# A two-block transformer kernel: the final norm and the next block's norm become one row, and column sums are asked for later

## The chip, the cores and the metric

The kernel runs on one core of one Trainium2 chip. The metric is the device time of one execution in microseconds. The core has five engines with their own instruction queues: PE (TensorE, matmuls out of SBUF into the eight banks of PSUM), DVE (VectorE), ACT (ScalarE), POOL (GpSimd) and SP, which here only issues DMAs. Engines are ordered against each other by semaphores: an instruction waits until a counter has reached a value, and everything behind it on its engine waits with it.

## The reference, cut to what matters

x has T = 512 tokens of D = 1024 features. The first block is an FFN, a mixer of attention and a linear recurrence, and a second FFN, each ahead of an RMS norm, and one final norm. The second block normalises that result once more and projects it ten ways.

```python
def rmsnorm(x, g):
    y = x * rsqrt(mean(x * x, axis=-1) + EPS)
    return y * g
...
x = x + 0.5 * swiglu_ffn(rmsnorm(x, ffn1_norm), ...)
x = x + hybrid_mixer(rmsnorm(x, mix_norm), ...)
x = x + 0.5 * swiglu_ffn(rmsnorm(x, ffn2_norm), ...)
x = rmsnorm(x, final_norm)          # the first block's result
...
h = rms_norm(x, norm_pre_g)         # the second block
u_a, z_a, q, k, v, o, z_b, gates, g_a, g_b = split(h @ w_in)
y_a = pool_mix(multiscale_pool(u_a)) * pool_scale * silu(z_a)
q, k = silu(conv5(q, k))
hb = mlstm(q, k, v, gates) + flip(mlstm(flip(...)))
y_b = rms(hb) * mlstm_norm_g * sigmoid(o) * silu(z_b)
merged = sigmoid(g_a + b_a) * (y_a @ w_proj_pool) + sigmoid(g_b + b_b) * (y_b @ w_proj_mlstm)
return x + rms_norm(merged @ w_out, norm_post_g)
```

## The kernel before

**Layout.** Everything is held transposed: features on the 128 partitions in 8 chunks, the 512 tokens along the row. So a norm's sum over features goes across partitions. It is done by ACT squaring the chunks into `scr`, DVE adding them (`add_square`, L1518, or `norm_sum`, L1506), PE turning the sums into four columns by narrow matmuls with a column of ones (`add_squares`, L494), ACT taking the root, DVE the reciprocal (`r_col`), and PE spreading it again as a row over all partitions (`spread_columns`, L501), which ACT copies to `r_row`.

**Weight units.** All weights come as 262 units of 128x1024 fp32 (512 KB). For each, SP issues the DMA (L414), ACT rounds it to `w_hi` (`head`, L1067), POOL subtracts for the rest `w_lo` (L432), and PE runs 24 matmuls of 128x512 columns: hi times hi, hi times lo, lo times hi over 8 chunks (`tile_unit`, L486 to L488; in the FFNs' second half `down`, L566 to L568). Each of the three buffers has two slots, so ACT's copy for unit u + 2 waits until PE has ended unit u. The stream x is split alike into `h_hi` (ACT, L1086) and `h_lo` (DVE, L1513).

**Norms 0 to 2** (before FFN1, the mixer, FFN2) multiply only the gain onto the stream; the root row is multiplied onto the results as they leave PSUM (L1552, L1556 in the FFNs). PE runs the first unit of the stage, then the column sums, the second unit, the row of roots, and goes on. **Norms 3 and 4** (the final norm, and the second block's) are done in full before PE goes on: x times gain times row (DVE, L2118), again squares, pair sums on POOL (L457), sums, root, row, and the normalised stream's split by DVE (L1539, L1535) and POOL (L450). Then the gates unit runs.

**Second block, in program order.** The gates unit (rows of gate values for the recurrence, prefix scans on DVE, L1805 ff.); `mlstm(0)`: ten head units whose results ACT copies out of PSUM (`take`, L1333), four convolutions on DVE (L1884, L1886) each followed by ACT's activation (L1341); a loop of three rounds `mlstm(h)`, in which the recurrence of head h - 1 (scores, eight steps with `c_state`, L1950, `roots`, `gated`, `y_tail`, L1988) runs between the ten units of head h; a last round with eight gate units (U_GB, L1402) between; `merge_b` (8 units); `pooled` (8 units for u, L1439, 8 for z, L1445, 2 for the mixing, L1019); `merge_a` (16); `output` (8, L2078). The order on each engine is written out by hand in these functions; nothing reorders it. Then the post norm (norm 5) of the output, and DVE (L2086, L2093) and POOL (L472, the first five chunks) multiply and add it to x, which SP writes out in eight DMAs.

## Time and profile before

| | |
|---|---|
| median of 3 runs | 1795.54 us (1794.02 to 1796.08) |
| the profiled execution, its own time | 1797.42 us |
| its span, first to last instruction | 1795.6 us |
| busy: PE, DVE, POOL, ACT | 1693.2, 700.0, 656.1, 623.7 us |
| mean granted TensorE clock | 0.969 |
| read from HBM | 144.86 MB, 82 GB/s over the span |

PE is busy 94% of the span. A busy time is a sum of the engine's instructions; where PE has a gap, the profile names what released it. The clock is the share of full speed (2.4 GHz) that was granted; it has two levels, 1.00 and 0.5, and a value between is a mean over a stretch. Matmul starts at full clock follow each other by 0.227 us, each shown with 0.39 us since they overlap.

### The profile page before, as it was taken

How to read it: one execution, taken by the hardware profiler on the slowest of the kernel's cores; microseconds unless marked ns; L12 is line 12 of the kernel's file. 1: busy time of each engine (PE TensorE's matmuls, PEld its weight loads, DVE VectorE, ACT ScalarE, POOL GpSimd, SP SyncE). 2: the span in 40 equal slices, each digit the busy share in tenths (PEclk: the TensorE clock that was granted, in tenths of full speed). 3: DMA queues.
4: the chain of work that ended last, by engine and by line, in shares of the span. 5: the costliest groups of instructions: out<-in, count | busy, mean ns of one | idle time of the engine just before them, and what ended most of it. 6: DMA issues, size and time to landing. Idle time of an engine off the chain costs nothing.

```text
span 1795.6 us, 22547 instructions
## 1 busy us (share of the span) xinstructions
PE 1693.2 (94%) x7996; PEld 1384.5 (77%) x7996; DVE 700.0 (39%) x1157; ACT 623.7 (35%) x917; POOL 656.1 (37%) x281
## 2 busy tenths in 40 slices
PE   6999999999999999999999988889898999999997
PEld 5888888778886678888888877677677778877876
DVE  4333330225326744333330127473736331463223
ACT  4332231234236653223321234334343423234431
POOL 2444444433330024444444434222222223444443
PEclk9999999999999999999999989899999999999998
DMA  3322232233220002222222222121111112322221
GB/s 145 103 95 93 94 103 95 94 140 94 82 82 25 2 33 85 94 97 101 93 93 96 103 71 71 59 71 59 58 58 58 58 59 82 117 93 88 100 94 70
DMA packets 41663, 148.68 MB, mean 83 GB/s; under 512 B 4624, under 2 KB 4752, under 8 KB 41360
## 3 DMA queue, kind: packets, MB, share of 16 engines
q1 hardware_dynamic: 40112, 142.36, 23.4%
q10 hardware_dynamic: 1504, 5.66, 1.0%
q8 instruction: 32, 0.52, 0.1%
q14 instruction: 15, 0.12, 0.0%
HBM read 144.86 MB, written 2.10 MB: 82 GB/s over the span
## 4 chain that ended last, share of the span: by engine, by line
PE 47%; issue 39%; POOL 9%; DVE 3%; ACT 1%; POOLq 0%; DVEq 0%; ACTq 0%
PE ps L486 10%; PE ps L488 10%; PE ps L487 10%; POOL w_lo L432 9%; PE ps L566 3%; PE ps L568 3%; PE ps L567 3%; PE ps L724 1%; PE ps L494 1%; PE ps L736 1%; PE ps L746 1%; PE ps L501 1%; DVE scr L1518 1%; PE ps L647 0%; DVE scr L2068 0%
## 5 line engine op out<-in xcount | busy, mean ns | idle before, releaser
L432 POOL TENSOR_TENSOR w_lo<-w_raw,w_hi 128x1024 fp32r<-128x1024 f32 x262 | 636.1, 2428 | 1001.9 <-ACT w_hi L1067 992.4
L486 PE MATMUL ps<-h_hi,w_hi 128*128 128x512 f32 x1504 | 600.6, 399 | 25.7 <-POOL w_lo L432 20.7
L1067 ACT ACTIVATE w_hi<-w_raw 128x1024 fp32r<-128x1024 f32 x260 | 275.5, 1060 | 945.5 <-PE ps L488 763.5
L487 PE MATMUL ps<-h_lo,w_hi 128*128 128x512 f32 x1504 | 592.0, 394 | 0.0
L488 PE MATMUL ps<-h_hi,w_lo 128*128 128x512 f32 x1504 | 591.6, 393 | 0.0
L486 PEld LDWEIGHTS ps<-h_hi,w_hi 128*128 128x128 f32 x1504 | 287.2, 191 | 90.8 <-issue 22.1
L488 PEld LDWEIGHTS ps<-h_hi,w_lo 128*128 128x128 f32 x1504 | 286.3, 190 | 61.1
L487 PEld LDWEIGHTS ps<-h_lo,w_hi 128*128 128x128 f32 x1504 | 286.8, 191 | 58.9
L566 PE MATMUL ps<-hid_hi,w_hi 128*128 (+1 forms) x352 | 137.2, 390 | 1.8 <-POOL w_lo L432 1.8
L567 PE MATMUL ps<-hid_lo,w_hi 128*128 (+1 forms) x352 | 136.9, 389 | 0.0
L568 PE MATMUL ps<-hid_hi,w_lo 128*128 (+1 forms) x352 | 136.9, 389 | 0.0
L1556 DVE TENSOR_TENSOR silu<-ps,r_row 128x512 f32<-128x512 f32 x44 | 30.4, 692 | 205.7 <-PE ps L488 201.8
L1571 DVE SCALAR_TENSOR_TENSOR x<-ps,x 128x512 f32<-128x512 f32 x16 | 11.0, 690 | 207.4 <-PE ps L568 207.4
L1561 DVE TENSOR_TENSOR hid_lo<-hid,hid_hi 128x512 f32 x44 | 71.1, 1615 | 40.1 <-ACT hid_hi L1116 40.1
L566 PEld LDWEIGHTS ps<-hid_hi,w_hi 128*128 128x128 f32 x352 | 66.1, 188 | 15.8 <-issue 2.2
L567 PEld LDWEIGHTS ps<-hid_lo,w_hi 128*128 128x128 f32 x352 | 66.1, 188 | 13.8
L568 PEld LDWEIGHTS ps<-hid_hi,w_lo 128*128 128x128 f32 x352 | 66.1, 188 | 13.8
L1886 DVE SCALAR_TENSOR_TENSOR scr<-qk_pad,param,scr 128x512 f32<-128x512 f32 x64 | 60.0, 938 | 7.7 <-DVE scr L1884 1.8
L1552 DVE TENSOR_TENSOR silu<-ps,r_row 128x512 f32<-128x512 f32 x44 | 30.4, 691 | 71.2 <-PE ps L488 54.1
L486 PE MATMUL ps<-y_hi,w_hi 128*128 128x512 f32 x128 | 50.0, 391 | 0.8 <-DVE y_lo L2043 0.7
L487 PE MATMUL ps<-y_lo,w_hi 128*128 128x512 f32 x128 | 49.8, 389 | 0.0
L488 PE MATMUL ps<-y_hi,w_lo 128*128 128x512 f32 x128 | 49.8, 389 | 0.0
(291 smaller groups left out, 1653.0 us busy)
## 6 DMA issues: line engine op xcount, KB each, us to landing
w_raw<-in_units SPq DMA_DIRECT2D x262, 512.0 KB, 3.2
x<-in_x SPq DMA_DIRECT2D x4, 512.0 KB, 7.1
w<-in_w ACTq DMA_DIRECT2D x1, 2048.0 KB, 8.1
out<-x SPq DMA_DIRECT2D x8, 256.0 KB, 2.0
scr<-proj ACTq DMA_DIRECT2D x8, 128.0 KB, 2.4
inv_count<-in_inv_count ACTq DMA_DIRECT2D x1, 1024.0 KB, 5.1
const<-in_const SPq DMA_DIRECT2D x1, 770.0 KB, 10.3
q_sc<-in_row_const ACTq DMA_DIRECT2D x1, 512.0 KB, 3.6
```

Source lines behind the costliest of these rows:

```text
L432: nc.gpsimd.tensor_tensor(w_lo[:, slot, :], w_raw[:, slot, :], w_hi[:, slot, :].bitcast(F32), ALU.subtract).then_inc(w_lo_done, 1)
L486: nc.tensor.matmul(ps[:, bank, :], whi, hi[:, k, :], start=(n == 0), stop=False)
L487: nc.tensor.matmul(ps[:, bank, :], whi, lo[:, k, :], start=False, stop=False)
L488: mm = nc.tensor.matmul(ps[:, bank, :], wlo, hi[:, k, :], start=False, stop=(n == DC - 1))
L566: nc.tensor.matmul(acc, w_hi[:, slot, at:at + P], mv_hi, start=start and kk == 0, stop=False)
L567: nc.tensor.matmul(acc, w_hi[:, slot, at:at + P], mv_lo, start=False, stop=False)
L568: mm = nc.tensor.matmul(acc, w_lo[:, slot, at:at + P], mv_hi, start=False, stop=stop and kk == 1)
L1067: nc.scalar.activation(w_hi[:, slot, :], w_raw[:, slot, :], ACT.Copy).then_inc(w_hi_done, 1)
L1552: nc.vector.tensor_tensor(silu[:, f, :], ps[:, 4 + 2 * f, :], r_row[:, :], ALU.mult).then_inc(scaled_done, 1)
L1556: chain.link(nc.vector.tensor_tensor(silu[:, f, :], ps[:, 5 + 2 * f, :], r_row[:, :], ALU.mult))
L1561: nc.vector.tensor_tensor(hid_lo[:, at, :].rearrange("p a t -> p (a t)"), hid[:, f, :], hid_hi[:, at, :].rearrange("p a t -> p (a t)").bit ...
L1886: ins = nc.vector.scalar_tensor_tensor(acc, tap, w, acc, ALU.mult, ALU.add)
```

## The change

In seven parts:

1. **Start.** The first gains come in a DMA of their own, and ACT loads its function table by a dummy copy before the data arrive. PE's first unit runs its w_hi matmuls first and w_lo's behind them.
2. **Norms 0 to 2.** PE runs two units before the column sums (in FFN and mixer), and a third before the row of roots. In the FFN's second half ACT copies w_hi for the next unit ahead of the squares, and the half-way sums on PE go.
3. **Norms 3 and 4** are one: the stream of the second FFN's result is x times the product of both gains (`both_col`), and the row for it is worked out from two sets of column sums, of the squares and of the squares weighed with the final gain's square (`root_of_both`, `inverse_of_both`). POOL's part in the norm goes.
4. **Second block's results.** Each leaves PSUM by a DVE multiply with the row (`take`, `take_gate`), ACT's functions then work in SBUF in place.
5. **x for the residual.** The normalised x, no longer formed above, is made in `pooled`: ACT multiplies a chunk with the gain, PE transposes it, ACT copies it back as token rows with the tokens' factor.
6. **Output** is computed with the tokens on the partitions: blocks of `m_hi`, `m_lo` are the stationary side and untiled w_out the moving one, over all eight banks, the chunk outermost.
7. **Post norm** is then a sum along the row: ACT squares with an accumulated sum, root, DVE reciprocal and multiply with a row of gains. POOL adds six pieces instead of five.

The diff, cut to its core:

```diff
@@ PE
+            def first_unit(bank, chunks):
+                pe.wait_ge(w_hi_done, 1)
...
             def column_sums(n):
                 pe.wait_ge(sqsum_done, n + 1)
...
+                bank = 5 if n == 3 else 0
+                mm = add_squares(bank, 0, scr[:, 0, :], True, True)
+                if n == 3:
+                    mm = add_squares(bank, TT, r_row, False, True)
+                mm.then_inc(ssq_done, 1)
...
-                            if first and f == 0:
-                                (row_of_roots if m else column_sums)(norm_of)
+                            if first and (f, m) == (0, 1):
+                                column_sums(norm_of)
+                            elif first and (f, m) == (1, 0):
+                                row_of_roots(norm_of)
...
-                if sums_inside:
-                    squares_of_half(norm_of + 1, True)
...
-                    if u == 0:
+                    if u == 1:
                         column_sums(1)
-                    elif u == 1:
+                    elif u == 2:
                         row_of_roots(1)
...
             def pooled():
-                with pe.Fori(0, DC) as i:
+                for j in range(DC):
+                    pe.wait_ge(ev_done, EV_POOL + j + 1)
+                    tile_unit(unit(U_POOL + j), 2 + j % 2, h_hi, h_lo)
...
+                    pe.wait_ge(xg_done, j + 1)
+                    for tt in range(TT):
+                        mm = nc.tensor.transpose(ps[:, 4 + j % 4, tt * P:(tt + 1) * P], x[:, j, tt * P:(tt + 1) * P], ident)
+                    mm.then_inc(xt_ready, 1)
...
             def output():
+                for k in range(DC):
+                    u, _, slot = unit(U_OUT + k)
+                    pe.wait_ge(w_lo_done, u + 1)
+                    pe.wait_ge(m_lo_done, k + 1)
+                    for tt in range(TT):
...
-            norm(3, "before")
-            norm(4, "last")
             gates()
@@ ACT
                 streams(0, 4)
+                head(unit(ud + kps + 2))
                 squares(norm_of + 1, 0, 4)
-                head(unit(ud + kps + 2))
...
                 for j in range(DC):
                     head(unit(U_POOL + j + 2))
...
-                    nc.scalar.activation(u_pad[:, j % 2, 8:8 + T], ps[:, 2 + j % 2, :], ACT.Copy).then_inc(ev_done, 1)
+                    nc.scalar.activation(x[:, j, :], x[:, j, :], ACT.Copy, scale=p_("g_final", j, j + 1)).then_inc(xg_done, 1)
                     if j >= 1:
                         pool_head(j - 1)
+                    act.wait_ge(xt_ready, j + 1)
+                    for tt in range(TT):
+                        at = slice(tt * P, (tt + 1) * P)
+                        ins = nc.scalar.activation(x[:, j, at], ps[:, 4 + j % 4, at], ACT.Copy, scale=x_col[:, tt:tt + 1])
...
+                for tt in range(TT):
+                    act.wait_ge(out_done, tt + 1)
+                    nc.scalar.activation(merged[:, 2 * (tt % 2):2 * (tt % 2) + 2, :], ps[:, 2 * tt:2 * tt + 2, :], ACT.Square,
+                                         accum_out=g_col[:, tt:tt + 1]).then_inc(osq_done, 1)
@@ DVE
+                def take(j):
+                    dve.wait_ge(unit_done, U_HEADS + HEAD_UNITS * h + j + 1)
...
+                    nc.vector.tensor_tensor(dst, ps[:, head_bank(j, not core), :], r_row[:, :], ALU.mult).then_inc(ev_done, 1)
...
+                between = take if units else lambda j: [take_gate(i) for i in GATE_B_AT[j]]
...
+                between(3)
+                step(0)
...
+                gated()
+                run(not units, (take_gate, 6), (take_gate, 7))
+                y_tail()
...
+                for n, (tt, half) in enumerate(PIECES):
...
+                    nc.vector.scalar_tensor_tensor(scr[:, n, :], ps[:, n, :], r_col[:, tt:tt + 1], g_row[:, half * T:(half + 1) * T],
                                                    ALU.mult, ALU.mult).then_inc(sum_done, 1)
```

**DVE, end of `mlstm(0)`**, the head units' stage between the gate scans and the loop. L1884 and L1886 (L1921 and L1923 after) are a convolution, L1895 (L1932) a product of gates, L1863 to L1868 (L1878 to L1883) the gate rows' products and columns. Before:

```order
L1858 TENSOR_SCALAR q_sc<-q_sc 64x512
L1884 TENSOR_SCALAR scr<-qk_pad,param 128x512 [waits qk_done,ev_done]
L1886 SCALAR_TENSOR_TENSOR scr<-qk_pad,param,scr 128x512 [waits dve_chain] x4
L1884 TENSOR_SCALAR scr<-qk_pad,param 128x512 [waits qk_done,ev_done]
L1886 SCALAR_TENSOR_TENSOR scr<-qk_pad,param,scr 128x512 [waits dve_chain] x4
L1895 TENSOR_TENSOR merged<-merged,scr 128x512 [waits ev_done]
```

After:

```order
L1873 TENSOR_SCALAR q_sc<-q_sc 64x512
L1904 TENSOR_TENSOR scr<-ps,r_row 128x512 [waits unit_done]
L1921 TENSOR_SCALAR scr<-qk_pad,param 128x512 [waits qk_done,ev_done]
L1923 SCALAR_TENSOR_TENSOR scr<-qk_pad,param,scr 128x512 [waits dve_chain] x4
L1904 TENSOR_TENSOR merged<-ps,r_row 128x512 [waits unit_done] x2
L1921 TENSOR_SCALAR scr<-qk_pad,param 128x512 [waits qk_done,ev_done]
L1923 SCALAR_TENSOR_TENSOR scr<-qk_pad,param,scr 128x512 [waits dve_chain] x4
L1904 TENSOR_TENSOR scr<-ps,r_row 128x512 [waits unit_done]
```

The evictions (L1904) of units 6 and 7 stand between the third and the fourth convolution, which came one behind the other before.

**ACT in `pooled`**, one of the eight u units. L1067 (L1088 after) is the w_hi copy for the unit after next, L1430 (L1444) the split of a pooled chunk. Before:

```order
L1067 ACTIVATE w_hi<-w_raw 128x1024 [waits unit_done,raw_full0]
L1439 ACTIVATE u_pad<-ps 128x512 [waits pool_done,unit_done]
L1430 ACTIVATE y_hi<-scr 128x512 [waits pool_done]
L1067 ACTIVATE w_hi<-w_raw 128x1024 [waits unit_done,raw_full1]
L1439 ACTIVATE u_pad<-ps 128x512 [waits pool_done,unit_done]
```

After:

```order
L1088 ACTIVATE w_hi<-w_raw 128x1024 [waits unit_done,raw_full0]
L1448 ACTIVATE x<-x,param 128x512
L1444 ACTIVATE y_hi<-scr 128x512 [waits pool_done]
L1454 ACTIVATE x<-ps,x_col 128x128 [waits xt_ready]
L1454 ACTIVATE x<-ps,x_col 128x128 x3
L1088 ACTIVATE w_hi<-w_raw 128x1024 [waits unit_done,raw_full1]
```

The eviction of u has left ACT; the scaled copy of x stands behind the w_hi copy, and PE's transposes wait for it; the copies back wait for PE.

**DVE in the head loop**, from the end of the third convolution to the first step's state copy (`c_state`). Before:

```order
L1886 SCALAR_TENSOR_TENSOR scr<-qk_pad,param,scr 128x512
L1901 ISA
L1902 REGISTER_ALU [waits cadd_ready]
L1902 TENSOR_SCALAR k_w<-k_tok,wk_tok 128x256
L1946 ISA [waits cadd_ready]
L1950 COPY c_state<-ps 128x257 [waits num_ready]
```

After:

```order
L1923 SCALAR_TENSOR_TENSOR scr<-qk_pad,param,scr 128x512
L1891 REGISTER_ALU
L1895 REGISTER_ALU [waits unit_done]
L1904 TENSOR_TENSOR qk_pad<-ps,r_row 128x512 [waits conv_done]
L1938 ISA
L1939 REGISTER_ALU [waits cadd_ready]
L1939 TENSOR_SCALAR k_w<-k_tok,wk_tok 128x256
L1983 ISA [waits cadd_ready]
L1987 COPY c_state<-ps 128x257 [waits num_ready]
```

The fourth eviction (unit 3 of the next head) stands between the third convolution and the step; three more stand ahead of earlier parts of the round.

## Rows read from the trace of the kernel before

**Rows 1.** The page, part 1: engine, busy us, share of the span, instructions
```profile
PE 1693.2 (94%) x7996; PEld 1384.5 (77%) x7996; DVE 700.0 (39%) x1157; ACT 623.7 (35%) x917; POOL 656.1 (37%) x281
```

**Rows 2.** Windows by stage: start:end and length, busy us (instructions), clock, DMA
```profile
1059.21:1088.18 28.97, 19.21 (x94) 16.43 (x92) 18.14 (x29) 12.39 (x21) 10.27 (x7) 0.65 0.07 21
1088.18:1162.42 74.24, 64.07 (x271) 51.62 (x272) 43.46 (x56) 30.72 (x39) 24.52 (x11) 0.91 0.24 78
...
1248.41:1338.94 90.53, 79.55 (x348) 65.69 (x349) 46.43 (x99) 31.75 (x46) 24.07 (x10) 0.94 0.17 58
...
1541.45:1631.93 90.48, 87.70 (x385) 71.78 (x384) 48.41 (x47) 31.45 (x42) 39.69 (x17) 1.00 0.32 109
...
1776.66:1795.60 18.94, 6.43 (x47) 6.05 (x47) 9.46 (x13) 0.89 (x2) 6.61 (x5) 0.62 0.30 111
```

**Rows 3.** Windows over single units and behind gaps, same columns
```profile
395.78:402.88 7.10, 7.10 (x27) 5.80 (x28) 0.18 (x1) 0.27 (x1) 0.00 (x0) 0.79 0.17 61
702.02:709.33 7.31, 7.31 (x28) 5.89 (x28) 0.18 (x1) 0.26 (x1) 1.50 (x1) 0.77 0.37 133
335.69:342.50 6.81, 6.81 (x30) 5.66 (x31) 0.00 (x0) 1.04 (x1) 2.26 (x1) 1.00 0.47 154
1145.36:1152.20 6.84, 6.84 (x23) 5.53 (x24) 0.00 (x0) 0.77 (x2) 2.37 (x1) 0.75 0.45 156
```

**Rows 4.** Timeline of the start: start us, us, engine line, what [idle before]
```profile
9.47 7.77 DVE L1513 SCALAR_TENSOR_TENSOR h_lo<-x,param,h_hi 128x512 fp32r<-128x512 f32 x6 [0.67 <-ACT h_hi L1086]
...
24.44 1.86 PE L494 MATMUL ps<-const,scr 128*128 128x1 f32 x8 [4.92 <-DVE scr L1518]
```

**Rows 5.** Timelines of PE at the first half-way step and two norms
```profile
335.69 0.49 PE L566 MATMUL ps<-hid_hi,w_hi 128*128 x1 [1.83 <-POOL w_lo L432]
...
394.66 1.26 PE L494 MATMUL ps<-const,scr 128*128 128x1 f32 x8 [4.28 <-DVE scr L1518]
...
701.11 1.05 PE L494 MATMUL ps<-const,scr 128*128 128x1 f32 x8 [1.18 <-DVE scr L1518]
```

**Rows 6.** Timelines of DVE, PE and ACT at the opening head units
```profile
1131.75 5.07 DVE L1886 SCALAR_TENSOR_TENSOR scr<-qk_pad,param,scr 128x512 f32<-128x512 f32 x4
...
1135.63 0.77 PE L486 MATMUL ps<-h_hi,w_hi 128*128 128x512 f32 x1 [5.89 <-POOL w_lo L432]
...
1141.75 1.04 ACT L1067 ACTIVATE w_hi<-w_raw 128x1024 fp32r<-128x1024 f32 x1
...
1145.36 0.47 PE L486 MATMUL ps<-h_hi,w_hi 128*128 128x512 f32 x1 [2.22 <-POOL w_lo L432]
```

**Rows 7.** Groups of instructions by form: busy us, mean ns, idle before
```profile
L432 POOL TENSOR_TENSOR w_lo<-w_raw,w_hi 128x1024 fp32r<-128x1024 f32 x262 | 636.1, 2428 | 1001.9 <-ACT w_hi L1067 992.4 <-ACT w_hi L1471 9.5
...
L1561 DVE TENSOR_TENSOR hid_lo<-hid,hid_hi 128x512 f32 x44 | 71.1, 1615 | 40.1 <-ACT hid_hi L1116 40.1
...
L1556 DVE TENSOR_TENSOR silu<-ps,r_row 128x512 f32<-128x512 f32 x44 | 30.4, 692 | 205.7 <-PE ps L488 201.8 <-ACT ps L1112 4.0
...
L1079 ACT ACTIVATE scr<-x 128x512 f32<-128x512 f32 x40 | 23.2, 619 | 5.1 <-DVE x L1571 2.6 <-DVE x L2118 2.3
```

**Rows 8.** Timeline of PE in the head loop, first round
```profile
1283.48 2.05 PE L947 MATMUL ps<-v_aug,k_w 128*128 128x257 f32 x4 [5.24 <-DVE c_state L1950]
```

**Rows 9.** Timelines of PE and DVE in the last round
```profile
1491.17 1.03 PE L967 MATMUL ps<-const,h_sum 128*128 128x128 f32 x8
...
1493.69 1.35 DVE L1988 TENSOR_TENSOR y_lo<-yb,y_hi 128x512 fp32r<-128x512 f32 x2
```

**Rows 10.** Timelines of ACT and PE at the end of pooling
```profile
1630.29 1.06 ACT L1067 ACTIVATE w_hi<-w_raw 128x1024 fp32r<-128x1024 f32 x1 [3.90 <-PE ps L488]
...
1631.93 0.47 PE L1019 MATMUL ps<-y_hi,w_hi 128*128 128x512 f32 x1 [1.74 <-issue]
```

**Rows 11.** Timelines of PE and POOL at the output stage and the tail
```profile
1732.82 0.50 PE L486 MATMUL ps<-m_hi,w_hi 128*128 128x512 f32 x1 [1.71 <-DVE merged L2030]
...
1784.52 6.61 POOL L472 TENSOR_TENSOR x<-x,scr 128x512 f32<-128x512 f32 x5 [15.11 <-DVE scr L2086]
```

More of the change, by code:

```diff
@@ L165, in build, with weight @@
         ident, ones = c_("ident"), c_("ones")
+        g_both, g_square = both_col[:, 0:DC], both_col[:, DC:2 * DC]
+        def weight(name, c):
+            return g_both[:, c:c + 1] if name == "both" else p_(name, c, c + 1)
         ffn = ExitStack()
@@ L247, in build @@
         m_lo = sb("m_lo", [P, DC, T], F32R, second)
+        g_row = sb("g_row", [P, D], F32, second)
         second.close()
@@ L1085, in raw_head @@
                     act.wait_ge(x_in[c // 2], 16)
-                nc.scalar.activation(h_hi[:, c, :], x[:, c, :], ACT.Copy, scale=p_(gain, c, c + 1)).then_inc(raw_hi_done, 1)
+                nc.scalar.activation(h_hi[:, c, :], x[:, c, :], ACT.Copy, scale=weight(gain, c)).then_inc(raw_hi_done, 1)
             def root(n):
@@ L1125, in streams @@
                 def streams(lo, hi):
-                    if gain is not None:
-                        for c in range(lo, hi):
-                            raw_head(norm_of + 1, c, gain)
+                    for c in range(lo, hi):
+                        raw_head(norm_of + 1, c, gain)
                 with act.Fori(0, kps // 2) as i:
@@ L1141, in ffn @@
                 load_root()
-                if gain is not None:
-                    streams(4, 8)
-                    head(unit(ud + 2 * kps + 1))
-                    squares(norm_of + 1, 4, 8)
-                else:
-                    squares(norm_of + 1, 4, 8)
-                    head(unit(ud + 2 * kps + 1))
+                streams(4, 8)
+                head(unit(ud + 2 * kps + 1))
+                squares(norm_of + 1, 4, 8)
             def project():
@@ L1482, in _ @@
             to_stream(U_MIXOUT, 2, "g_ffn2")
-            ffn(U_FFN2, 1, 2, None)
-            norm(3, parts=False)
-            squares(4, 0, 8)
-            norm(4)
+            act.wait_ge(both_done, 1)
+            ffn(U_FFN2, 1, 2, "both")
             gates()
@@ L1994, in run @@
                         part(*arg)
-                run(core, (keys,), (decays, 0))
+                if not core:
+                    take(0)
+                    take(1)
+                    convolve(0)
+                    take(2)
+                    gates()
+                    convolve(1)
+                    take(3)
+                    take(4)
+                    row_ends()
+                    take(5)
+                    convolve(2)
+                    take(6)
+                    take(7)
+                    convolve(3)
+                    take(8)
+                    row_columns()
+                    gate_product(0)
+                    take(9)
+                    gate_product(1)
+                    return
@@ L2002, in mlstm @@
                 run(units, (convolve, 2))
[L2003 removed]
+                between(3)
+                step(0)
+                step(1)
                 run(units, (convolve, 3))
[L2005 to L2009 removed]
+                between(4)
+                step(2)
@@ L2010, in mlstm @@
+                step(3)
+                between(5)
+                step(4)
+                between(6)
+                step(5)
+                between(7)
+                step(6)
+                step(7)
+                between(8)
+                run(units, (gate_product, 0), (take, 9))
+                roots()
                 run(units, (gate_product, 1))
-                run(core, (gated,), (y_tail,))
+                gated()
+                run(not units, (take_gate, 6), (take_gate, 7))
```

433 lines of the change are left out of this document (227 added, 206 removed).

## The prediction

> **What bounds the kernel now.** The first table of the page comes first [rows 1]: PE is busy 1693.2 of the 1795.6 us of the span. So the time is PE's, and a change can win only the stretches in which PE waits, or matmuls it no longer issues. The windows by stage [rows 2] show where it waits: 9.8 us from the end of the second FFN to the end of the gates unit, and the clock there is 0.65; 10.2 us in the stage behind it; 11.0 in one round of the head loop; 2.8 in the pooling stage; 12.5 behind the last weight unit. The timelines of the groups behind them then name what each wait ends with. One weight unit is 24 matmuls and takes 5.44 us at full clock: 24 steps of 0.227 (30 matmuls in the window of 6.81 us at clock 1.00 [rows 3]); the windows over two units in which the clock was at the lower of its two levels (1.2 of 2.4 GHz) for a part [rows 3] give 7.10 and 7.31 us.
>
> The sum is made against the profiled execution, 1797.42 us with a span of 1795.6; the median of the runs shown, 1795.54, is 1.9 lower, and the result is moved by that.
>
> **Column sums later (norms 0 to 2).** Before, PE asks for the summed squares right behind the first unit of a stage. At the start it waits 4.92 us for DVE's adds [rows 4], and the unit behind runs partly at the half clock, as the two of [rows 3] do. Asked one unit later, the sums, ready at 24.4, fall inside a unit that ends near 25.4. The unit 0 itself gains nearly nothing from needing only w_hi, since DVE's six h_lo operations (7.77 us from 9.47) [rows 4] feed it either way. 4.92, some 2.1 for the unit and about 0.2 for the narrow matmuls at the slow clock give **-7.2** (bounds -5 and -8.5: the second the 1.28 us that the table load is taken ahead of the data). The same edit before the mixer: gap 4.28 [rows 5], unit 7.10 [rows 3], 4.28 + 1.66 = 5.9, with the shorter matmuls in clock **-6.1**. Before the second FFN: 1.18 [rows 5] + 1.87 [rows 3], **-3.2**. The two half-way steps of the FFN: w_hi of the next unit is copied before the squares, so the 1.83 us wait for w_lo in the first FFN goes [rows 5] (from the second, which has none, nothing): with the short clock of its first matmuls **-2.0**; the eight narrow matmuls inside FFN2, 1.05 us at a like place [rows 5], of which the weight loads of neighbours hide a part, go: **-0.8**. Together -19.3.
>
> **Final norm and pre-norm as one.** From the end of the second FFN (1059.21) to the first matmul of the head loop (1162.42) the old program takes 103.2 us, of which the two norms and the gates unit are 28.97 [rows 2], where a lone unit is 5.44. So 23.5 us are there to win. I expect nearly all to be given back. The chain behind is DVE's: it now does everything that it did (convolutions, gate scans, 43.46 us busy in the 74.24 [rows 2]) and ten evictions more, and the only work it lost are the two norms' multiplies. An eviction with the row is a product with one operand in PSUM; the nearest row is the FFN's, 692 ns [rows 7], so 10 x 0.69 = 6.9 us. Before, head unit 7 started at 1135.63 after a wait of 5.89 us and unit 8 at 1145.36 [rows 6], 86.2 us behind the FFN's end. Both waited for w_lo, that is for ACT's w_hi, which stood in ACT's queue behind the activation of a convolution, and so for DVE. After, the column sums are late too: PE asks for them behind the first head unit, DVE has them some 14.6 us behind the FFN's end, and the first evictions wait for the row. Walked through operation by operation with the durations of the trace, unit 7 starts at 66 us and ends at 71.4. Its eviction now stands ahead of the last convolution in DVE's queue, which before ran without it. From there: eviction 0.7; convolution 0.5 and 5.07 (the last one of before); from its end to ACT's next w_hi, with activation, table load and row exponentials, 4.9 (1136.8 to 1141.75 [rows 6]); w_hi 1.04; w_lo 2.43 [rows 7]: 86.0, unit 8 no sooner than before, unit 9 at 96 behind the turned rows, and the head loop 101.5 us behind the FFN: **-1.7**. The bounds are wide: -12 (half of the 23.5 kept) and +6.
>
> **The head loop.** Ten results per round leave PSUM on DVE instead of ACT. ACT's copy was off the path. On DVE four of the 0.69 us evictions stand ahead of the first step of the recurrence, which already waits 5.24 us for DVE (c_state) at 1283.48 [rows 8], and DVE is continuously busy in the 24 us before. 4 x 0.69 = 2.8, less about 0.6 for convolutions that then meet POOL at another time: **+2.2** a round, bounds 1.9 and 3.1; three rounds, **+6.6**. The boundary between rounds waits for yb and sees no more, since the later six evictions lie where DVE has idle time (46.43 busy in 90.53 [rows 2]). In the last round the y_tail comes behind the eviction of the eighth gate unit, which ends with the stage itself. Before, the two y_lo operations started at 1493.69, 4 us ahead of that end [rows 9]. After: eviction 0.7, two y_lo of 0.69, the second of which meets POOL's w_lo (2.43 us [rows 7]), so **+5**, bounds 2 and 6.
>
> **Pooling.** This is the largest cost. Behind each of eight units PE must transpose a chunk of x, and waits for ACT's x times g_final. ACT issues that behind the w_hi copy of the unit after next, which in turn waits for this unit's last matmul: nothing can be early. The copy is 1.06 us [rows 10], the next operation overlaps it by 0.1; the scaled copy from SBUF is 0.62 (the nearest row, L1079 [rows 7]); with the start and the signals, some 0.4, the gap is 1.95 us, and four transposes of 128 columns take 0.44 (eight take 1.03 at 1491.17 [rows 9], the last one's end counted in). 8 x (1.95 + 0.44) = 19.1. The 1.74 us wait ahead of the mixing [rows 10] goes, since the last tail is long done, and with it the slower first matmuls behind it, about 2.1 in all; the evictions of u take a place among DVE's window sums, a unit ahead of their use: **+17.0**. Bounds: 14 (ACT ahead by a third of its copy) and, with the clock, 31 (below). The wait of 1.71 us between the merge and the output stage [rows 11] goes, since token blocks need m_lo chunk by chunk: **-1.9**.
>
> **The tail.** Before: 1776.66 to 1795.60, 18.94 us [rows 2]: 40 narrow matmuls, root, spread, DVE's eight products, POOL's adds, the transfer. After: nothing returns to PE. ACT squares a token block of 128x1024 with its sum (nearest row: w_hi of that size, 1.06 [rows 10], plus the read of the sum and the root: 1.5 each), DVE one reciprocal and two products per block (4 x 1.75, the last ends 4.5 us behind the last matmul), POOL's six adds (6.61 us for five before [rows 11]) and DVE's two run behind the products, to 6.7, and the last transfer takes 3.3, as the end of the span behind the last add does before: 10.0, **-8.9** (bounds -8 and -10).
>
> **Sum.** -19.3 - 1.7 + 6.6 + 5 + 17.0 - 1.9 - 8.9 = -3.2: 1794.2 for an execution like the profiled one, **1792.3** against the median.
>
> **Does moving evictions to DVE make them meet POOL?** In the rows, a product with both operands in SBUF has a mean of 1615 ns, and the one from PSUM 692 [rows 7], beside the same w_lo operations: only the former are held up. I therefore price all evictions at 0.69. [...] Here r_row is in SBUF and the other operand in PSUM. [...] Were the evictions held up like the former, those ahead of the recurrence and of the last convolution would cost up to 1 us more each, near +5 on the path in all.
>
> **Rivals.**
> *The clock falls in the pooling stage* (slower). Behind a lone gap of 1.83 us [rows 5] the granted clock is 1.00, behind one of 2.22 [rows 6] a stretch of 6.84 us is at 0.75 [rows 3]. The new gaps are 1.8 to 1.95, eight in a row, which no row shows. If they are answered as the 2.22 was, a unit costs 1.8 us more (7.31 [rows 3] against 5.44). All eight: +14, 1806; half: 1799. The Trainium skill, TensorE: Matmul & The Clock Gate, "HAM oscillation — how this bites in real kernels", describes this shape: bursts of matmuls with idle gaps in which the clock is throttled again in each round. By it the stage would cost 31 us in place of 17. For my case: the gap nearest in size kept the clock. Chance 0.2.
> *The norm's 23.5 us are kept by half or more* (faster): DVE is done sooner because its two-input SBUF operations meet POOL less often, and unit 8 comes at 78 us. Then -12 in place of -1.7: 1782 to 1786. For it: DVE is busy only 43.46 of 74.24 us there [rows 2]. Chance 0.15.
> *DVE's queue is the longer chain* (slower): an eviction waits for a unit that waits for an activation that waits for DVE's convolution, so each delay goes round; then the opening stage gives +6 and the loop 3.1 a round: 1803. Chance 0.12.
> *The start does not gain* since DVE's h_lo chain shifts the adds with it: +4, 1796; inside the case below.
>
> **How the numbers follow.** The case of the sum has 0.53 and, with terms uncertain by some 4 us, spreads 1786 to 1798. The range must leave out no more than 0.2: 1784 takes in most of the faster rival, 1805 most of the clock's and all of the queue's. A measurement of this kernel can tell about 0.2%, 3.6 us, from no change: 1791.9 to 1799.1. Faster: 0.53 x 0.46 + 0.15 = 0.39; slower: 0.53 x 0.04 + 0.2 x 0.8 + 0.12 x 0.9 = 0.29; the rest, 0.32, same.
>
> **What would show it.** The column sums of norms 0 to 2 without a wait ahead, and the units behind at 5.44; the head loop starting 101 us behind the FFN's end; the wait for c_state at 7 to 8 us; eight PE waits of 1.8 us on ACT's x in pooling, at clock 1.00; 10 us behind the last unit. Wrong would be: a PE clock under 1.00 in pooling, a y_lo wait over 6 us, or a head loop that starts before 95.

## The result and the profile after

The changed kernel is slower: 1816.92 us (1813.21 to 1819.37, four runs) against 1795.17 for the kernel before, a ratio of 1.012, interval 1.0101 to 1.0139. The profiled execution has a span of 1817.6 us against 1795.6. The forecast was 1792.3, its range 1784 to 1805: the time lies outside it, on the other side of no change.

The page of the changed kernel, parts 1 and 2; PE is busy 7.7 us more than in [rows 1], though it runs fewer matmuls:

```profile
PE 1700.9 (94%) x7924; PEld 1375.6 (76%) x7924; DVE 748.5 (41%) x1224; ACT 620.2 (34%) x922; POOL 650.4 (36%) x276
...
PEclk9999999999999899999999997899999999999999
```

The windows of the changed kernel by the same stages as [rows 2], with the columns of that group. From the first to the last: FFN2's end to the head loop, three rounds, the last round, merge_b, pooling, mixing with merge_a, output, tail:

```profile
1052.59:1156.01 103.42, 76.63 (x318) 61.62 (x317) 58.05 (x85) 32.91 (x43) 27.43 (x11) 0.83 0.19 64
1156.01:1248.69 92.68, 78.67 (x349) 64.28 (x348) 56.63 (x109) 29.73 (x41) 26.73 (x11) 0.95 0.19 63
1248.69:1341.59 92.90, 79.95 (x348) 65.71 (x349) 54.11 (x109) 28.99 (x40) 24.59 (x10) 0.92 0.17 56
1341.59:1433.84 92.25, 79.36 (x348) 65.22 (x348) 54.07 (x109) 28.95 (x39) 24.67 (x10) 0.93 0.16 57
1433.84:1504.75 70.91, 65.66 (x301) 54.34 (x301) 32.85 (x87) 27.71 (x39) 17.87 (x8) 0.98 0.14 49
1504.75:1551.20 46.45, 46.45 (x192) 37.28 (x193) 4.82 (x7) 7.43 (x7) 18.65 (x8) 0.96 0.25 88
1551.20:1661.37 110.17, 94.23 (x418) 75.61 (x416) 60.20 (x63) 41.03 (x73) 39.24 (x16) 0.98 0.27 94
1661.37:1762.32 100.95, 100.29 (x433) 81.10 (x434) 39.97 (x45) 43.57 (x50) 45.59 (x18) 1.00 0.26 90
1762.32:1807.45 45.13, 45.13 (x193) 35.97 (x191) 5.82 (x9) 13.63 (x19) 18.70 (x9) 1.00 0.19 67
1807.45:1817.58 10.13, 0.00 (x0) 0.00 (x0) 6.76 (x9) 1.44 (x4) 6.28 (x5) 0.74 0.55 207
```

The lengths of the same stages, with the forecast's terms beside them (us; the column of before is from its timeline by the same marks):

| stage | before | after | difference | forecast |
|---|---|---|---|---|
| start to FFN2's end | 1059.21 | 1052.59 | -6.6 | -19.3 |
| FFN2's end to the head loop | 103.21 | 103.42 | +0.2 | -1.7 |
| three rounds | 265.86 | 277.83 | +12.0 | +6.6 |
| last round | 69.51 | 70.91 | +1.4 | +5 |
| merge_b | 43.66 | 46.45 | +2.8 | 0 |
| pooling | 90.48 | 110.17 | +19.7 | +17.0 |
| mixing, merge_a, wait ahead of output | 100.89 | 100.95 | +0.1 | -1.9 |
| output | 43.84 | 45.13 | +1.3 | 0 |
| tail | 18.94 | 10.13 | -8.8 | -8.9 |
| sum | | | +22.0 | -3.2 |

Two things stand out. Stretches in which PE runs nothing but the matmuls of units became longer (merge_b, output, and the second halves of the two FFNs), and PE has no gap there. And two thirds of the gain forecast for the first part are missing. This is the window over the 22 units of the first FFN's second half in the changed kernel; before, the same 530 matmuls took 121.96 us with the 1.83 us wait of [rows 5] among them:

```profile
253.80:377.18 123.38, 123.38 (x530) 99.28 (x529) 16.98 (x19) 31.99 (x36) 52.85 (x22) 1.00 0.28 94
```

Clock 1.00, PE busy throughout, no wait: 123.38 / 22 = 5.61 us a unit instead of 5.44. The steps between the starts of those matmuls are 231, 232 and 237 ns (ahead of lo with w_hi, hi with w_lo and hi with w_hi), where before all are 227. Of the other units only those whose stream is o, y or m show it; those on h keep 227.

### The profile page after: what moved, and what is told of

It reads as the page before. It is cut to its first block, busy times and chain, and to the rows that moved or that the text cites. A ratio compares the mean times of both kernels' runs of the same rounds, so it can differ in the third digit from the quotient of the medians.

```text
span 1817.6 us, 22524 instructions
## 1 busy us (share of the span) xinstructions
PE 1700.9 (94%) x7924; PEld 1375.6 (76%) x7924; DVE 748.5 (41%) x1224; ACT 620.2 (34%) x922; POOL 650.4 (36%) x276
## 4 chain that ended last, share of the span: by engine, by line
PE 64%; issue 23%; POOL 6%; DVE 5%; ACT 1%; DMA 0%; DVEq 0%; POOLq 0%; SPq 0%; ACTq 0%
PE ps L487 14%; PE ps L489 14%; PE ps L488 14%; POOL w_lo L450 6%; PE ps L571 2%; PE ps L570 2%; PE ps L569 2%; PE ps L953 1%; PE ps L725 1%; PE ps L965 1%; PE ps L737 1%; PE ps L747 1%; DVE scr L1923 1%; PE ps L963 1%; PE ps L1056 1%
## 5 line engine op out<-in xcount | busy, mean ns | idle before, releaser
L1088 ACT ACTIVATE w_hi<-w_raw 128x1024 fp32r<-128x1024 f32 x260 | 275.6, 1060 | 1003.2 <-PE ps L489 781.8
L1923 DVE SCALAR_TENSOR_TENSOR scr<-qk_pad,param,scr 128x512 f32<-128x512 f32 x64 | 60.3, 942 | 8.3 <-DVE scr L1923 2.4
L953 PE MATMUL ps<-v_aug,k_w 128*128 128x257 f32 x96 | 28.5, 424 | 27.4 <-DVE c_state L1987 16.8
```

The lines of the kernel that those rows point to most:

```text
L953: mm = nc.tensor.matmul(ps[:, 4 + e, 0:VW], k_w[:, d, e * P:(e + 1) * P], v_aug[:, c, :], start=True, stop=True)
L1088: nc.scalar.activation(w_hi[:, slot, :], w_raw[:, slot, :], ACT.Copy).then_inc(w_hi_done, 1)
L1923: ins = nc.vector.scalar_tensor_tensor(acc, tap, w, acc, ALU.mult, ALU.add)
```

## The experiments

Twelve kernels. "The changed kernel" is the one of the diff. Each ratio is to the kernel before, run beside it, whose median was between 1795.2 and 1799.8 us; so between experiments the ratios are the safer comparison. Stage lengths and clocks are those of one profiled execution each.

### Where the tiles stand

The change adds two small tiles, x_col and both_col, ahead of hid_hi, o_hi, y_hi and m_hi (the streams that PE reads in the FFNs' second halves, in the attention's output, in both merges and in the output stage). Tiles are placed one behind the other, each size rounded up to 32 bytes; hid_hi moves by 96 bytes, w_hi, w_lo and h_hi stay.

```diff
         both_col = sb("both_col", [P, 2 * DC])
+        pad = sb("pad", [P, 8])
```

> The changed kernel with one more tile of 32 bytes per partition behind both_col, so that hid_hi, o_hi, y_hi and m_hi stand on a multiple of 64 bytes again (they are 32 bytes off in the changed kernel); nothing else differs. Theory of the address: the steps of the matmuls that read those tiles return from 231, 232 and 237 ns to 227. 1056 matmuls of the FFN halves at 6.7 ns on average are 7.0 us, 384 on y 2.5, 96 on o 0.6, 192 of the output stage 1.4: 11.5 us less, 1805.4. Rival, the step is longer because of what the other engines now do beside PE (evictions on DVE): no change, 1817, and the steps stay at 231 to 237.

Measured: 1818.22, ratio 1.0112 (1.0083 to 1.0142): no change. The same half FFN:

```profile
253.69:377.04 123.35, 123.35 (x530) 99.30 (x529) 16.97 (x19) 31.99 (x36) 52.87 (x22) 1.00 0.29 95
```

A miss: a multiple of 64 does not help. The steps are nearly even now, about 233 ns.

```diff
+        pad = sb("pad", [P, 8])
         spare = sb("spare", [P, 1])
```

> The kernel before with a tile of 32 bytes ahead of spare, so that the same tiles stand 32 bytes off a multiple of 64. Theory of the address: the FFN's second halves go from 5.44 to 5.60 us a unit, 44 units 7.0 us, y 2.5, o 0.6, m 1.3: 1795.2 + 11.4 = 1806.6. Rival (other engines' work): no change, 1795.

Measured: 1813.16, ratio 1.008 (1.0049 to 1.011), slower than before by more than the 11.4 expected (13.4 against the median of its own comparison, 1799.8). A window of 100 us inside the second FFN's second half, first the kernel before, then this one; the first figure in brackets is the number of PE's matmuls:

```profile
945.00:1045.00 100.00, 100.00 (x443) 82.81 (x442) 6.11 (x7) 21.45 (x23) 44.84 (x19) 1.00 0.28 95
```

```profile
955.00:1055.00 100.00, 100.00 (x430) 80.36 (x429) 6.11 (x7) 21.15 (x22) 42.57 (x18) 1.00 0.29 95
```

At clock 1.00 and with PE busy without a break, 430 matmuls instead of 443 fit in 100 us. So 32 unused bytes slow the kernel before, and no eviction or other work is needed for it: the place of the tiles is the cause. Whether it is a tile's own address or its distance from another, the next two tell:

```diff
         both_col = sb("both_col", [P, 2 * DC])
+        pad = sb("pad", [P, 40])
```

> The changed kernel with a tile of 160 bytes behind both_col. The tile of 32 bytes left the steps at 232 to 237 ns although hid_hi then stood on a multiple of 64 and of 128; in the kernel before, hid_hi, o_hi, y_hi, m_hi and w_hi all leave the same rest, 128, by 256. With 160 bytes they do so again (by 512 they do not). Theory of the rest by 256: steps of 227 ns, 11.5 us less than the changed kernel, 1.0056 of before. Rival, the rest by 512 or more decides: the steps stay at 232 to 237 and the time at 1.012 of before.

```diff
+        pad = sb("pad", [P, 8])
         x = sb("x", [P, DC, T])
```

> The kernel before with the tile of 32 bytes ahead of x, so that every tile moves by 32 bytes and the distance between weights and stream stays. Theory of the distance (what counts is where the moving tile stands against the weights): steps of 227 ns everywhere, no change of time. Rival, the address itself counts: all 1728 x 3 matmuls of units at 233 instead of 227, 34 us, and the FFN's halves 7 more: 1836.

Measured: 1811.73, ratio 1.0078 (1.0053 to 1.0104) for the first, 1796.53, ratio 1.0001 (0.9986 to 1.0017) for the second. The half FFN with 160 bytes, and the window of 100 us with all tiles shifted:

```profile
255.31:375.15 119.84, 119.84 (x530) 99.29 (x529) 16.90 (x19) 31.93 (x36) 52.69 (x22) 1.00 0.29 97
```

```profile
955.00:1055.00 100.00, 100.00 (x443) 82.81 (x442) 6.11 (x7) 22.02 (x23) 43.13 (x18) 1.00 0.30 100
```

119.84 us for the 530 matmuls, and 443 in the window: the fast step is back in both. What counts is the distance between the tile of the stream, which moves through PE, and the weights, which stand in it:

| kernel | hid_hi less w_hi, rest by 256 bytes | step |
|---|---|---|
| before; all tiles shifted by 32 | 0 | 227 ns |
| before, 32 ahead of spare | 32 | 233 |
| the changed one | 96 | 231 to 237 |
| the changed one + 32 | 128 | 233 |
| the changed one + 160 | 0 | 227 |

The output stage of the changed kernel has the roles turned round, m_hi stationary and w_hi moving, and the same distance of 96: 234 ns, and 227 with 160 bytes. Against the kernel with 160 bytes, the cost in the changed kernel is 2 x 3.54 us in the FFNs' halves, 1.2 in merge_b (the clock left out), 1.9 in the mixing and merge_a (100.95 us against 99.01), 1.4 in the output stage (45.13 against 43.68) and, from the steps, 0.6 on o: near 12 us of the 22. In time the 160 bytes took the ratio from 1.012 to 1.0078, some 8 us with an interval of 6 either way; in the profile its pooling stage had 3 us more than the changed kernel's (below).

### Pooling

```diff
                 for j in range(DC):
-                    head(unit(U_POOL + j + 2))
                     nc.scalar.activation(x[:, j, :], x[:, j, :], ACT.Copy, scale=...).then_inc(xg_done, 1)
+                    head(unit(U_POOL + j + 2))
```

> The changed kernel, with ACT's copy of x times g_final issued ahead of the w_hi copy of the unit after next in the eight u units of the pooling stage. Theory of the order: PE's eight waits of 1.82 to 1.91 us, 15.0 in all, and the short clock drop behind them (1.7) go, the transposes (0.65 each) stay: 1817 - 15 to 17 = 1800 to 1802. Rival, the wait only moves (POOL's w_lo or the copies back out of PSUM become late): half of it or less, 1810.

Measured: 1812.14 against 1799.8 before, ratio 1.0053 (1.0026 to 1.0079). The seven executions fall into two groups, three from 1803.2 to 1804.2 us with a mean clock of 0.970 and four near 1812.2 with 0.965; the profiled one is of the second. First ACT and PE in the changed kernel at the second of the eight waits, then the stage and a transpose with the copy ahead:

```profile
1564.88 1.06 ACT L1088 ACTIVATE w_hi<-w_raw 128x1024 fp32r<-128x1024 f32 x1 [4.38 <-PE ps L489]
1565.84 0.71 ACT L1448 ACTIVATE x<-x,param 128x512 f32<-128x512 f32 x1
...
1566.69 0.63 PE L1017 MATMUL ps<-const,x 128*128 128x128 f32 x4 [1.91 <-ACT x L1448]
```

```profile
1556.95:1654.15 97.20, 93.27 (x417) 76.07 (x416) 59.43 (x63) 40.47 (x73) 40.59 (x16) 0.98 0.32 106
...
1568.36 0.60 PE L1017 MATMUL ps<-const,x 128*128 128x128 f32 x4
1568.71 0.47 PE L487 MATMUL ps<-h_hi,w_hi 128*128 128x512 f32 x1
...
1618.64 0.49 PE L487 MATMUL ps<-h_hi,w_hi 128*128 128x512 f32 x1 [1.93 <-DVE silu_z L2149]
```

110.17 became 97.20: 13.0 us in the stage, of the 15.0 that the eight waits made up. The transposes no longer wait for anything, but PE now waits twice for an eviction on DVE, 1.06 us for u_pad and 1.93 for silu_z. These two waits, the transposes' own time (0.35 us from their first to the next unit, and 0.09 for that unit's longer first step) and one clock stretch are most of the 6.7 us that remain over before.

The clock was the first rival. Behind these gaps of nearly equal length it did fall, but not behind all eight. Five kernels have these waits and nothing else changed in the stage. In their profiles PE was at the lower level for 3.4 us (the changed kernel, 110.17, and the one of the next section), 6.8 (32 bytes, 111.76) and 10.2 (160 bytes, 113.28, and the one of the section on the head loop):

```profile
1544.72:1658.00 113.28, 97.33 (x418) 77.88 (x416) 60.15 (x63) 41.00 (x73) 39.37 (x16) 0.95 0.28 91
```

So one, two or three such stretches, each making the stage some 1.6 us longer; what decides the number, no run shows.
### The opening head units

```diff
-                    take(7)
                     convolve(3)
+                    take(7)
                     take(8)
```

> The changed kernel, with DVE's fourth convolution of the opening head units ahead of the eviction of unit 7 instead of behind it. Theory of the DVE queue: the convolution ends 12.9 us sooner (at 1116.6 instead of 1129.5), unit 8 starts right behind unit 7 instead of 12.8 us later, and the head loop starts 12 us sooner: 1805. Rival, the next wait (unit 9, the turned rows, the first round's wait for c_state) takes it back: 5 us or less, 1812.

Measured: 1803.6, ratio 1.003 (1.0015 to 1.0046), 0.9 percent under the changed kernel's. First the changed kernel, PE ahead of units 7 and 8 and DVE between, then this one's stage and the same two waits:

```profile
1116.67 0.77 PE L487 MATMUL ps<-h_hi,w_hi 128*128 128x512 f32 x1 [7.96 <-POOL w_lo L450]
...
1125.30 0.69 DVE L1904 TENSOR_TENSOR merged<-ps,r_row 128x512 f32<-128x512 f32 x1 [12.30 <-PE ps L489]
...
1126.42 3.11 DVE L1923 SCALAR_TENSOR_TENSOR scr<-qk_pad,param,scr 128x512 f32<-128x512 f32 x4
...
1138.05 0.77 PE L487 MATMUL ps<-h_hi,w_hi 128*128 128x512 f32 x1 [12.79 <-POOL w_lo L450]
```

```profile
1049.77:1139.82 90.05, 73.70 (x316) 59.58 (x316) 60.16 (x85) 32.91 (x43) 27.47 (x11) 0.89 0.22 74
...
1113.84 0.77 PE L487 MATMUL ps<-h_hi,w_hi 128*128 128x512 f32 x1 [7.95 <-POOL w_lo L450]
...
1124.35 0.47 PE L487 MATMUL ps<-h_hi,w_hi 128*128 128x512 f32 x1 [2.36 <-POOL w_lo L450]
```

In the changed kernel DVE idles 12.30 us for unit 7 with a convolution ready behind it. With the two turned round the stage is 90.05 instead of 103.42: the 13.4 us that the merged norm gains there had been lost to this one place in a queue.

### The head loop

```diff
-                run(units, (convolve, 2))
                 between(3)
                 step(0)
                 step(1)
-                run(units, (convolve, 3))
+                run(units, (convolve, 2))
                 between(4)
                 step(2)
                 step(3)
+                run(units, (convolve, 3))
```

> The changed kernel; in the three rounds of the head loop DVE's third and fourth convolutions come behind the first two and the next two steps of the recurrence instead of ahead of them. Theory of the DVE queue: PE's wait for c_state (4.17, 5.84, 5.82 us) shrinks by the convolution's 4.4 us, so 4 us a round and 12 in all, to 1805. Rival, the third convolution is then late for ACT's activation and the next w_hi, and PE waits for w_lo instead: 3 us or less in all.

Measured: 1802.87, ratio 1.0039 (1.0021 to 1.0057). The changed kernel's wait in the second round (the first round has 3.75 and 4.17 one behind the other), then two rounds of this one and its first round's waits:

```profile
1285.53 2.05 PE L953 MATMUL ps<-v_aug,k_w 128*128 128x257 f32 x4 [5.84 <-DVE c_state L1987]
```

```profile
1152.29:1236.64 84.35, 75.34 (x350) 61.86 (x348) 54.51 (x109) 29.73 (x41) 27.46 (x11) 0.99 0.22 68
1236.64:1324.08 87.44, 78.43 (x348) 64.80 (x349) 53.03 (x109) 28.99 (x39) 24.63 (x10) 0.95 0.18 61
...
1180.05 1.13 PE L953 MATMUL ps<-v_aug,k_w 128*128 128x257 f32 x4 [1.28 <-DVE d_mat L1973]
...
1183.25 1.10 PE L953 MATMUL ps<-v_aug,k_w 128*128 128x257 f32 x4 [1.63 <-DVE c_state L1987]
```

The rounds fall by 8.3, 5.5 and 4.3 us, in the first two with a clock of 0.99 and 0.95 instead of 0.95 and 0.92. The DVE queue was the cause, and no unit of the rounds had to wait for w_lo, as it would if ACT's activation had become late. In time it is 14 us of the 18; in this profile the opening stage was 1.6 and the pooling stage 3.2 us longer than the changed kernel's.

### All four together

This kernel has the three orders above and an unused tile of 416 bytes, with which the distance of the tiles is again a multiple of 256.

> The changed kernel with the copy of x ahead of w_hi in pooling (-13.0 in that stage), the fourth convolution ahead of unit 7's eviction (-13.4), the later convolutions of the loop (-12 if that theory holds) and a tile of 416 bytes that gives hid_hi, o_hi, y_hi and m_hi the rest by 512 that they have in the kernel before (-11.5). If the four causes are apart and additive: 1817 - 50 = 1767, 0.984 of before. If two of them share a wait: 1778.

Measured: 1765.66 (1760.01 to 1770.86), ratio 0.983 (0.9797 to 0.9863). Its opening stage, first round, pooling and tail:

```profile
1042.11:1135.92 93.81, 75.15 (x317) 61.12 (x317) 62.35 (x86) 32.96 (x43) 26.94 (x11) 0.87 0.22 72
1135.92:1223.87 87.95, 77.04 (x350) 62.96 (x348) 56.25 (x109) 29.73 (x41) 26.77 (x11) 0.96 0.20 66
...
1514.75:1610.41 95.66, 91.75 (x418) 74.91 (x416) 59.53 (x63) 40.44 (x73) 40.64 (x16) 1.00 0.33 109
1753.11:1763.38 10.27, 0.00 (x1) 0.00 (x0) 6.90 (x9) 1.45 (x4) 6.42 (x5) 0.68 0.54 204
```

51 us lie between the changed kernel and this one, where 50 were expected, and no matmul of the computation is different. So the causes add, as far as four executions from 1760 to 1771 us can tell. Of the 54 us between the two profiled spans, 5 are the clock of the attention, at its lower level for 13.7 us here and for 23.9 in the changed kernel's.

### One part of the change alone, and without the merged norm

```diff
-                            if first and f == 0:
-                                (row_of_roots if m else column_sums)(norm_of)
+                            if first and (f, m) == (0, 1):
+                                column_sums(norm_of)
+                            elif first and (f, m) == (1, 0):
+                                row_of_roots(norm_of)
```

and the same in the mixer, with ACT's copies of w_hi moved to match, and the one at the FFN's half ahead of the squares.

> The kernel before with one part of the change alone: in the FFNs and the mixer PE asks for the column sums behind the second unit and for the row of roots behind the third, and at the FFN's half ACT copies w_hi ahead of the squares. The start, the norms 3 and 4, the evictions, the pooling and the tail are those of before. If the changed kernel's gain ahead of the second FFN's end is this part's: the three waits of 4.92, 4.28 and 1.18 us with the slow units behind them and the 1.83 us wait go, 16 to 18 us, 1779, 0.991 of before. Rival, the clock takes part of it back later (in the attention its half-speed stretches differ by 14 us between runs): 8 us, 1788.

Measured: 1781.52, ratio 0.992 (0.9896 to 0.9944). It reaches the second FFN's end at 1045.52, 13.7 us sooner than before, and is 14 us faster in time: nothing behind takes the gain back. It is less than the 16 to 18 expected; apart from the stretch behind the norm that goes, its attention was at the lower clock level for 20.5 us against 13.7 before, which is 3.4 us.

With the loop's order in addition, in the kernel before's form:

> The kernel of the part alone, and in the head loop the two later convolutions behind the steps of the recurrence, as in the changed kernel's experiment. Nothing of the merged norm. If the loop's order is worth as much without the evictions on DVE: PE's waits for c_state of 4.21, 5.24 and 4.21 us fall by 3 each, 10 us with the clock, so 1769, 0.985 of before, about as fast as the mended changed kernel (0.983): then the merged norm with all that it moved brings nothing. If the order only pays where the evictions stand in the queue: 1778.

Measured: 1767.82 (1765.75 to 1770.02), ratio 0.9835 (0.9812 to 0.9858), not to be told from the mended changed kernel. Its opening stage and first round:

```profile
1049.42:1152.02 102.60, 82.79 (x365) 67.91 (x364) 61.57 (x85) 42.99 (x60) 34.87 (x17) 0.83 0.19 62
1152.02:1233.21 81.19, 74.63 (x349) 61.93 (x348) 43.32 (x98) 32.47 (x46) 27.04 (x11) 1.00 0.21 68
```

Stage by stage against the mended one: 7.3 us more up to the second FFN's end (the attention was at the lower clock level for 30.7 us against 13.7), 8.8 more in the opening stage, 9.3 more in the tail, 1.9 more ahead of the output; 6.8, 1.4 and 4.7 less in the rounds, 4.6 less in the last, 5.2 less in pooling. So the kernel with the merged norm is 9 us ahead where it replaces two norms, and 17.5 behind in the four rounds, in which DVE has the evictions. Some 8 of the 17.5 are clock (27.3 us at the lower level against 10.2); that the evictions are the cause of both is argued, since no run moves them back to ACT. The output with tokens on the partitions wins 11 and has a price in pooling.

The next kernel takes the output part onto that one, without the merged norm; x is normalised there already, so the transposes need no factor.

```diff
+                    for tt in range(TT):
+                        mm = nc.tensor.transpose(ps[:, 4 + j % 4, tt * P:(tt + 1) * P], x[:, j, tt * P:(tt + 1) * P], ident)
+                    mm.then_inc(xt_ready, 1)
...
+                    act.wait_ge(xt_ready, j + 1)
+                    nc.scalar.activation(x[:, j, :], ps[:, 4 + j % 4, :], ACT.Copy).then_inc(xt_done, 1)
```

> The kernel with late sums and late convolutions, not the merged norm, and of the change also the output stage with tokens on the partitions and the post norm along the row; x, which here is normalised already, is transposed in the pooling stage with nothing to wait for, and copied back by one ACT copy a chunk. If the parts add as the stages of the mended kernels say: transposes 8 x 0.65 = +5.2, the wait of 1.71 us ahead of the output stage with its slow start -1.9, the tail 19.6 against 10.2, -9.4: 6 us less than the 1767.8 without it, 1762, 0.980 of before. Rival, ACT's additional copy of 0.6 us a unit in the pooling stage makes w_hi late: 1766.

Measured: 1765.98 (1762.26 to 1766.46), ratio 0.9822 (0.9791 to 0.9852): inconclusive against the one without it. Its stages gain 8.8 us in all, more than the 6 expected: pooling is 93.02 against 90.49, so it pays 2.5 and not 5.2 for the transposes; the tail is 10.22 against 19.59, and the output starts 1.9 sooner. But its first and third round, whose code is the same, are 3.7 and 2.3 us longer than in the other's profile. DVE is busy there for 47.0 and 46.2 us against 43.3 and 42.3, and the first has a clock stretch that the other lacks; so the last 2 us between these kernels are not told apart by one profile each.

A last order in the mended kernel, with the third convolution and unit 5's eviction ahead of the row ends and the row exponentials behind one more w_hi:

```diff
                     take(4)
-                    row_ends()
                     take(5)
                     convolve(2)
+                    row_ends()
...
-                    if not core and j == 5:
+                    if not core and j == 6:
                         row_exponentials()
```

> The mended kernel, with the eviction of unit 5 and the third convolution of the opening head units ahead of the row ends on DVE, and on ACT the row exponentials behind the w_hi copy of the unit after. The mended kernel still waits 7.98 us ahead of unit 7 and 2.42 ahead of unit 8 for ACT's w_hi. If both come from that order: unit 7 starts with no wait and unit 8 some 4 us sooner, 4 to 6 us in all, 1760, 0.980 of before. Rival, the row exponentials become late for the turned rows ahead of unit 9: no change, 1766.

Measured: 1767.42, ratio 0.9831 (0.9808 to 0.9854): no change. PE's waits in the opening stage became one:

```profile
1120.71 0.76 PE L488 MATMUL ps<-h_hi,w_hi 128*128 128x512 f32 x1 [8.13 <-POOL w_lo L451]
```

Unit 7 has no wait, and unit 8 has 8.13 us, where there were 7.98 and 2.42. The stage is 1.9 us shorter, and the round behind it 1.3 longer: in time, no change, as the rival had it, though by the wait of unit 8, which now ends with POOL's w_lo, and not by the turned rows. What sets it was not tried.

## Why the prediction was wrong

**The step that failed** is one sentence ahead of the sum: "One weight unit is 24 matmuls and takes 5.44 us at full clock". The whole account of the change was made in waits and instructions, with that as a constant, and the diff's two new tiles had no term. They cost near 12 us, in six stretches of unit matmuls, where the profile shows no wait: a unit there takes about 5.6 us. That is half of the 25.2 between -3.2 and +22.0. Without it the time, some 1805, would have been at the range's end and still slower than before; the other half is the clock, the head loop and pooling, below.

**Column sums later (-19.3; measured -6.6).** The mechanism is right: the waits of [rows 4] and [rows 5] are gone, and the start gave 9.2, more than the 7.2, since PE begins at 7.21 us instead of 11.50. Alone, with the steps at 227 ns, the later sums gave 13.7. What is missing in the changed kernel is 7.7 for the steps (FFNs' halves and o) and 5.1 for the clock in the attention: apart from the stretch behind the norm, which the change took away as forecast, it was at its lower level for 23.9 us in this profile against 13.7 before. Over the executions profiled here that figure goes from 13.7 to 30.7 us, and differs between kernels with the same attention; it moves a total by up to 8.5 us, and a range of 4 us around a sum left it out.

**The merged norm (-1.7; +0.2).** The walk through the queue held: unit 7 was forecast 66 us behind the FFN's end and came at 64.1, unit 8 at 86.0 and came at 85.5, the loop at 101.5 and came at 103.4. The reason given, the eviction of unit 7 ahead of the last convolution, is shown by the experiment that turns them round (-13.4).

**The head loop (+6.6; +12.0).** The mechanism was right, the size not. The second and third round grew by 2.4 and 2.9 us, near the 2.2 of the forecast; the first by 6.7. There PE's wait of 4.21 us before became two, of 3.75 and 4.17, 3.7 us more, since beside the four evictions one more convolution met POOL: one of its operations took 2.90 us, beside a w_lo of 2.40, where the same operation of the next convolution took 0.75.

```profile
1178.61 2.90 DVE L1923 SCALAR_TENSOR_TENSOR scr<-qk_pad,param,scr 128x512 f32<-128x512 f32 x1 [0.15 <-DVE scr L1921]
...
1186.85 0.75 DVE L1923 SCALAR_TENSOR_TENSOR scr<-qk_pad,param,scr 128x512 f32<-128x512 f32 x1 [0.15 <-DVE scr L1921]
```

And the first round was at the lower clock level for 9.8 us against 3.4 before, another 3 us. The term of the head loop had no clock in it.

**The last round (+5; +1.4).** Over-sized: y_lo does not meet POOL as feared; PE waits 2.30 us for it.

```profile
1503.10 1.28 DVE L2025 TENSOR_TENSOR y_lo<-yb,y_hi 128x512 fp32r<-128x512 f32 x2
...
1504.75 0.49 PE L487 MATMUL ps<-y_hi,w_hi 128*128 128x512 f32 x1 [2.30 <-DVE y_lo L2025]
```

But the lower clock level follows into merge_b, some 1.6 of its 2.8 us; the rest are the steps.

**Pooling (+17.0; +19.7).** The gaps are 1.82 to 1.91 us, near the 1.95 computed. The four transposes are as computed too: their records show 0.60 to 0.66 us, but overlap with the next unit, and by the steps they cost 0.44. The experiment confirms the waits as the main part; the change did not need them. Over the forecast came one stretch at the lower clock level, 1.6 us, and the wait ahead of the mixing, which was to go and went from 1.74 only to 0.94:

```profile
1661.37 0.47 PE L1037 MATMUL ps<-y_hi,w_hi 128*128 128x512 f32 x1 [0.94 <-issue]
```

**The tail (-8.9; -8.8)** went as said. So did the 1.71 us ahead of the output: with 160 bytes the stage with the mixing and merge_a is 99.01 us, 1.9 less than before; in the changed kernel the longer steps on y eat them up (+0.1).

**Evictions and POOL.** All evictions took 0.69 us in the changed kernel, beside POOL's operations too. So the price drawn from [rows 7] holds. The Trainium skill, SBUF — State Buffer, "SBUF: two separate sides", has the rule for it: DVE and GpSimd share a pair of ports as an exclusive lock, and a DVE operation needs it in a 2-port performance mode or with two SBUF inputs. An eviction has one input in SBUF and one in PSUM, and none of the 73 in the second block took longer than 0.70 us; the trace agrees.

The rivals: none of the four had the mechanism that decided. That of the clock was true in part (one to three stretches of the eight), and the sign named for it, a PE clock under 1.00 in pooling, did show: 0.98. That of DVE's queue as the longer chain was true in the loop only. The norm's gain was not kept, and the start did gain.

## What to carry to other kernels

A new small tile moves every tile allocated behind it. Compare the addresses, or the steps between matmul starts of one and the same line, before reading anything into an order of work. Where an engine's queue holds an operation that waits for a late unit, look for what stands ready behind it: moving one convolution was worth 13 us here and two others 14, each more than the 9 us by which the merged norm is ahead in its own stage.

## What the runs showed of the hardware

In this kernel matmuls of rounded fp32 tiles (fp32r) with 512 columns follow each other by 227 ns at full clock where the distance between the moving and the stationary tile within a partition is a multiple of 256 bytes, and by 231 to 237 ns at the three other rests tried (32, 96, 128). It does not matter where both stand: shifting all tiles by 32 bytes left the steps and the time as they were (ratio 1.0001). The busy time of PE hides it, since each matmul is shown longer (389 against 392 to 399 ns) and no gap appears. Why, no run tells; nor was another rest, type or width tried.

Eight gaps of 1.8 to 1.9 us in a row brought PE to the lower clock level for 3.4 to 10.2 us in five profiles with the same pooling code, and never behind each gap; each 3.4 us at that level made the stage some 1.6 us longer.
